# Sample attention of a two-layer decoder step: the value pages from the third on are issued from ACT's DMA queue instead of SP's

## The chip, the cores and the metric

The kernel runs on one core of a Trainium2 chip. The metric is the device time of one execution in microseconds, lower is better. Instructions are written out for each engine: PE (TensorE), DVE (VectorE), ACT (ScalarE), POOL (GpSimd) and SP (SyncE, which here only issues DMAs). Every engine takes its own instructions in order, and engines wait for each other through semaphores.

## The reference

One inference step over a prompt of 512 tokens and eight sample sequences of four new tokens, model width 2048. Layer 0 is a gated linear recurrence, layer 1 a stick-breaking attention with 16 heads, 4 key and value heads and head size 128. The sample sequences attend to 1024 past tokens each, whose keys and values lie in a paged pool; the page table says which eight pages of 128 tokens belong to a sequence.

```python
past_k = cache_k[page_table].reshape(Bs, n_pages * PAGE_SIZE, KV_HEADS, HEAD_DIM)
past_v = cache_v[page_table].reshape(Bs, n_pages * PAGE_SIZE, KV_HEADS, HEAD_DIM)
...
z = jnp.einsum('bqkgd,bskd->bkgqs', qb, k).astype(jnp.float32) / math.sqrt(HEAD_DIM)
z = z + bias.astype(jnp.float32)[None, :, :, None, None]
log_keep = jnp.where(mask, jax.nn.log_sigmoid(-z), 0.0)
suffix = lax.cumsum(log_keep, axis=4, reverse=True) - log_keep
attn = jnp.where(mask, jnp.exp(jax.nn.log_sigmoid(z) + suffix), 0.0)
o = jnp.einsum('bkgqs,bskd->bqkgd', attn.astype(v.dtype), v)
```

The suffix sum runs from the newest token back, so the pages are taken from the newest to the oldest.

## The kernel before

The dense layers come first and last: SP loads weight tiles, ACT and DVE split them into a high and a low part, PE multiplies in three passes (L610 to L612). Between the attention of the prompt and the output projection stands the sample attention, with all eight sequences together. It is the part that the change touches.

The sample attention is a loop of 16 turns, written out, over half pages: turn j works on page n = j // 2 + 1, counted from the newest, and on sequences 0 to 3 (even j) or 4 to 7 (odd j), so on four pages of 128 tokens by 512 numbers. Every engine has its own version of the loop, and stages of different turns stand side by side in it (four turns follow for the tail). Per turn:

- PE transposes four key pages (`key_turn`, L849), each followed by the scores of an earlier one (`scores`, L863), then multiplies the weights of turn j - 4 with its four value pages (`values`, L887) and transposes the weights of turn j - 3 (`weights_turn`, L882). The key pages 4j + 2 to 4j + 5 are transposed in turn j; for 4j + 2 PE needs ACT's copy of page 4j.
- ACT copies even key pages from PSUM to SBUF (`key_copy`, L1219, pages 4j and 4j + 2), does the absolute value, the exponential and the logarithm of turn j - 1 (L1222, L1223, L1226), the exponential of the weights of turn j - 2 (`weight_exp`, L1232), and copies the transposed weights of turn j - 3 from PSUM (`weight_copy`, L1237).
- DVE copies the odd key pages (L1694), scales the logits (L1720) and does the suffix sum (L1725 to L1733).

Pages are kept in two slots (n % 2) for keys (`KPG`) and for values (`VPG`). SP issues all page loads, 256 KB each, four in a group, one group for each half page. For each load it reads the page's number from SBUF into a register (`value_load`, L452) and issues the DMA (L454). The keys and values of pages 1 and 2 are issued first, 32 loads. From page 3 on a key group waits until PE has transposed the half page that it overwrites (`kp_t`), and a value group until PE has multiplied the one that it overwrites (`d_pv`); key groups and value groups alternate, the values two pages behind the keys. `d_pv` counts two for the new tokens and then one for each finished half page of values. After the pages SP goes on with the weights of the output projection (`load_pair_e`, L439).

On ACT two waits ahead of one activation become a semaphore instruction of its sequencer for one and a wait held by the activation for the other; the profile shows it on the line of the second `wait_ge` (L1218, L1236).

Of the kernel before, what the change touches and what calls it, by code (L numbers as in the profile page):

```python
# [33 lines left out]
NB, NT = 8, 4  # L34
# [14 lines left out]
NPAGE = 8  # L49
# [53 lines left out]
def build(nc, a, out):  # L103
    ctx = ExitStack()
    with ctx:
        def sem(name):
            return ctx.enter_context(nc.semaphore(name))
# [4 lines left out]
        def sb(name, shape, dt=F32, offset=None):  # L112
            size = 4
            for n in shape[1:]:
                size *= n
            if offset is None:
                offset = at[0]
                at[0] += (size + 31) // 32 * 32
            return nc.alloc_sbuf_tensor_at(name, list(shape), dt, offset=offset), offset
# [23 lines left out]
        PT, _ = sb("PT", [1, NB * NPAGE], I32)  # L143
# [3 lines left out]
        KPG, _ = sb("KPG", [P, 2, NB, KVW], offset=U_AT)  # L147
        VPG, _ = sb("VPG", [P, 2, NB, KVW], offset=U_AT + 2 * NB * KVW * 4)
# [23 lines left out]
        pt_in = sem("pt_in")  # L172
# [40 lines left out]
        keys_in = [[sem(f"keys_in{n}{h}") for h in range(2)] for n in range(2)]  # L213
        values_in = [[sem(f"values_in{n}{h}") for h in range(2)] for n in range(2)]
# [18 lines left out]
        d_pv = sem("d_pv")  # L233
# [51 lines left out]
        NHALF = 2 * NPAGE  # L285
# [49 lines left out]
        def _(sp):  # L335
# [103 lines left out]
            def load_pair_e(i, strips=(0, 1)):  # L439
                for s in strips:  # L440
                    for u in range(2):
                        load_unit(i * 4 + (E0 + 2 * s + u), u,
                                  w_out_b[:, u * UT:(u + 1) * UT, bass.ds(i * 2 * P + s * P, P)])
# [3 lines left out]
            sp.wait_ge(pt_in, 16)  # L447
            sp.wait_ge(unit_done, E0)

            def load_pages(n, h, pages, cache, arrived):  # L450
                for b in range(h * NB // 2, (h + 1) * NB // 2):
                    page = sp.value_load(PT[0:1, b * NPAGE + NPAGE - n:b * NPAGE + NPAGE - n + 1], min_val=0,  # L452
                                         max_val=cache.shape[0] - 1)
                    sp.dma_start(pages[:, n % 2, b, :], cache[bass.ds(page, 1)].rearrange("o s k d -> s (o k d)"))\  # L454
                        .then_inc(arrived[n % 2][h], 16)

            def load_keys(n, h):
                if n > 2:
                    sp.wait_ge(kp_t, 8 * (n - 3) + 4 * h + 4)
                load_pages(n, h, KPG, a["cache_k"], keys_in)  # L460

            def load_values(n, h):
                if n > 2:
                    sp.wait_ge(d_pv, 2 * (n - 3) + h + 3)
                load_pages(n, h, VPG, a["cache_v"], values_in)

            for n in range(1, 3):
                for h in range(2):
                    load_keys(n, h)
            for n in range(1, 3):  # L470
                for h in range(2):
                    load_values(n, h)
            for n in range(3, NPAGE + 3):
                for h in range(2):
                    if n <= NPAGE:
                        load_keys(n, h)
                    if n > 4:
                        load_values(n - 2, h)
            load_pair_e(0, (1,))
            with sp.Fori(1, KD // 2) as i:  # L480
                load_pair_e(i)
# [484 lines left out]
        def _(act):  # L966
# [248 lines left out]
            def key_copy(c):  # L1215
                act.wait_ge(kp_t, c + 1)
                if c >= 4:
                    act.wait_ge(kp_used, c - 3)  # L1218
                nc.scalar.activation(KPT[:, c % 4, :], KT[:, c % 2], ACT.Copy).then_inc(kp_even, 1)  # L1219

            def one_plus_exp(src, tile):
                steps.done(nc.scalar.activation(tile, src, ACT.Abs))  # L1222
                steps.done(nc.scalar.activation(tile, tile, ACT.Exp, scale=-1.0))  # L1223

            def log_of(tile):
                nc.scalar.activation(tile, tile, ACT.Ln, bias=1.0).then_inc(d_l, 1)  # L1226

            def weight_exp(j):
                act.wait_ge(d_arg, j + 2)
                if j >= 2:  # L1230
                    act.wait_ge(d_wt, j)
                nc.scalar.activation(DW[j % 2], DZ[j % 2], ACT.Exp).then_inc(d_exp, 1)  # L1232

            def weight_copy(j):
                act.wait_ge(d_wt, j + 2)
                act.wait_ge(d_pv, j + 1)  # L1236
                nc.scalar.activation(WPT[:, j % 2, :], WT[:, j % 2], ACT.Copy).then_inc(d_wt_out, 1)  # L1237

            act.wait_ge(d_zout, 1)
            one_plus_exp(new_z, new_l)  # L1240
            log_of(new_l)
            for j in range(NHALF + 4):
                if j < NHALF:
                    key_copy(4 * j)
                if j == 0:
                    act.wait_ge(d_arg, 1)
                    nc.scalar.activation(new_w, new_arg, ACT.Exp).then_inc(d_exp, 1)
                if 1 <= j <= NHALF:
                    act.wait_ge(d_zout, j + 1)
                    if j >= 3:  # L1250
                        act.wait_ge(d_scan, j - 2)
                    one_plus_exp(DZ[(j - 1) % 2], DL[(j - 1) % 2])
                if j < NHALF:
                    key_copy(4 * j + 2)
                if 1 <= j <= NHALF:
                    log_of(DL[(j - 1) % 2])
                if j == 0:
                    act.wait_ge(d_wt, 1)
                    act.wait_ge(d_cleared, 1)
                    for h in range(2):  # L1260
                        nc.scalar.activation(WPT[0:NS, h, :], WT[0:NS, h], ACT.Copy).then_inc(d_wt_out, 1)
                if 2 <= j <= NHALF + 1:
                    weight_exp(j - 2)
                if 3 <= j <= NHALF + 2:
                    weight_copy(j - 3)
            act.wait_ge(d_pv, NHALF + 1)
            nc.scalar.activation(OE[0], OS[:, 0], ACT.Copy).then_inc(d_sums[0], 1)

# [547 lines left out]
```

## Time and profile before

| | us |
|---|---|
| median of 3 runs | 1953.79 |
| lowest, highest | 1953.53, 1960.9 |
| profiled execution | 1958.79 |
| its span | 1957.1 |
| PE busy in the span | 1766.8 (90%) |
| DVE, ACT busy | 1124.3 (57%), 805.7 (41%) |
| page loads, keys and values | 64 + 64 of 256 KB |
| sample attention, first key copy to last value product | 1585.9 to 1709.6 |

Times in the views are microseconds from the span's start. Busy times count an engine's own work; register operations, semaphore waits and DMA issues belong to its sequencer and are shown with a q (SPq, ACTq). The granted clock is given as a share of 2.4 GHz, so 0.50 is 1.2 GHz.

### The profile page before, as it was taken

To read this page: it belongs to the slowest core of one execution; us is meant where nothing else is said; L and a number is where in the kernel's file an instruction comes from. 1 tells how busy PE (TensorE), PEld (TensorE's weight loads), DVE (VectorE), ACT (ScalarE), POOL (GpSimd) and SP (SyncE) were. 2 spreads that over 40 slices of the span, in tenths; PEclk is the share of its full clock that TensorE was granted. 3 is DMA by queue.
4 is the path that set the end of the run, shared out by engine and by line. 5 is a ranking of instruction groups with operands and counts; after the bars stand their busy time and mean duration, and the time that the engine had idled before them with its cause. 6 is when DMAs were issued, how large, how long until landed. Compare 5 with 4: busy or idle time off the path is not lost.

```text
span 1957.1 us, 36289 instructions
## 1 busy us (share of the span) xinstructions
PE 1766.8 (90%) x13985; PEld 1695.8 (87%) x13985; DVE 1124.3 (57%) x1854; ACT 805.7 (41%) x1174; POOL 267.4 (14%) x181
## 2 busy tenths in 40 slices
PE   4899999999997999975889999999999878699995
PEld 3899999999997999974889998999999745499993
DVE  4756565676656222249467666757757757542226
ACT  3344434334445222223255555546545645432212
POOL 3200000000000001014322232232232100001110
PEclk9999999999998999995999999999999979999995
DMA  5332322232221323335312222222222367723324
GB/s 196 94 90 87 93 86 86 86 96 86 75 86 38 92 86 91 91 95 166 92 55 76 66 78 65 65 79 75 65 77 65 98 204 225 229 65 86 86 87 160
DMA packets 278709, 191.67 MB, mean 98 GB/s; under 512 B 7899, under 2 KB 250715, under 8 KB 277979
## 3 DMA queue, kind: packets, MB, share of 16 engines
q1 hardware_dynamic: 277708, 188.03, 32.5%
q0 software_dynamic: 896, 2.23, 0.4%
q8 instruction: 67, 1.10, 0.2%
q14 instruction: 38, 0.31, 0.0%
HBM read 174.26 MB, written 15.97 MB: 97 GB/s over the span
## 4 chain that ended last, share of the span: by engine, by line
PE 71%; DVE 12%; issue 7%; ACT 7%; SPq 2%; DMA 1%; POOL 0%; ACTq 0%; DVEq 0%; POOLq 0%
PE PS L610 20%; PE PS L611 20%; PE PS L612 20%; PE PS L849 1%; PE Z L610 1%; PE Z L611 1%; PE Z L612 1%; DVE Y L1525 1%; ACT L1160 1%; ACT WS L975 1%; DVE T L1567 1%; SPq L452 1%; DMA prow<-in_state_h_dram 1%; DVE T L1565 1%; ACT T L1107 1%
## 5 line engine op out<-in xcount | busy, mean ns | idle before, releaser
L610 PE MATMUL PS<-U,WS 128*128 128x272 f32 x3712 | 1086.6, 293 | 58.9 <-DVE U L1532 34.2
L611 PE MATMUL PS<-U,WS 128*128 128x272 f32 x3712 | 1087.3, 293 | 0.0
L612 PE MATMUL PS<-U,WS 128*128 128x272 f32 x3712 | 1084.8, 292 | 0.0
L610 PEld LDWEIGHTS PS<-U,WS 128*128 128x128 f32 x3712 | 713.4, 192 | 66.3 <-issue 34.3
L612 PEld LDWEIGHTS PS<-U,WS 128*128 128x128 f32 x3712 | 712.8, 192 | 0.0
L611 PEld LDWEIGHTS PS<-U,WS 128*128 128x128 f32 x3712 | 711.3, 192 | 0.8
L1303 DVE TENSOR_TENSOR WS<-raw,WS 128x1024 fp32r<-128x1024 f32 (+1 forms) x240 | 304.5, 1269 | 507.4 <-ACT WS L975 504.9
L975 ACT ACTIVATE WS<-raw 128x1024 fp32r<-128x1024 f32 (+1 forms) x240 | 246.6, 1028 | 605.4 <-PE PS L612 602.0
L527 POOL TENSOR_TENSOR raw<-raw,GN 128x1024 f32<-128x1024 f32 x80 | 160.0, 2000 | 433.5 <-DMA raw<-in_b_w_in_dram 337.7
L539 POOL TENSOR_TENSOR T<-T 128x544 f32<-128x544 f32 x60 | 88.4, 1474 | 379.4 <-ACT T L1071 376.9
L536 POOL COPY T<-T 128x544 f32<-128x544 f32 x4 | 3.0, 744 | 808.8 <-ACT T L1071 781.7
L849 PE MATMUL PS<-IDN,KPG 128*128 128x128 f32 x256 | 45.1, 304 | 21.9 <-ACT KPT L1219 17.6
L1578 DVE TENSOR_TENSOR T<-T,Z 128x256 f32<-128x256 f32 (+1 forms) x64 | 33.3, 520 | 50.9 <-PE Z L749 50.8
L849 PEld LDWEIGHTS PS<-IDN,KPG 128*128 128x128 f32 x256 | 29.4, 151 | 36.1 <-ACT KPT L1219 21.0
L1071 ACT ACTIVATE T<-Y 128x544 f32<-128x544 f32 (+1 forms) x48 | 31.1, 648 | 71.6 <-DVE Y L1503 71.6
L1106 ACT ACTIVATE T<-T 128x256 f32<-128x256 f32 (+1 forms) x64 | 31.7, 495 | 64.8 <-DVE T L1551 64.7
L1134 ACT ACTIVATE U<-T 128x256 fp32r<-128x256 f32 (+1 forms) x64 | 31.9, 499 | 62.9 <-DVE T L1567 62.9
L1124 ACT ACTIVATE U<-T 128x256 fp32r<-128x256 f32 (+1 forms) x64 | 31.7, 495 | 60.9 <-DVE T L1583 60.9
L1572 DVE TENSOR_TENSOR U<-T,U 128x256 fp32r<-128x256 f32 (+1 forms) x64 | 43.3, 677 | 14.9 <-ACT U L1134 14.5
L1398 DVE SCALAR_TENSOR_TENSOR T<-T,CH 128x512 f32<-128x512 f32 x60 | 45.1, 752 | 8.4 <-DVE T L1396 2.9
L770 PE MATMUL Z<-U,KVP 128*128 128x256 f32 (+1 forms) x64 | 24.1, 377 | 27.3 <-DVE U L1588 24.5
L1503 DVE COPY Y<-PS 128x544 f32 (+1 forms) x32 | 23.1, 721 | 41.1 <-PE PS L612 41.1
(221 smaller groups left out, 1972.8 us busy)
## 6 DMA issues: line engine op xcount, KB each, us to landing
raw<-in_a_w_in_dram SPq DMA_DIRECT2D x80, 512.0 KB, 3.8
raw<-in_b_w_in_dram SPq DMA_DIRECT2D x64, 512.0 KB, 4.0
raw<-in_a_w_out_dram SPq DMA_DIRECT2D x32, 512.0 KB, 3.9
raw<-in_b_w_out_dram SPq DMA_DIRECT2D x32, 512.0 KB, 4.0
KPG<-in_cache_k_dram SPq DMA_DIRECT2D x64, 256.0 KB, 3.0
VPG<-in_cache_v_dram SPq DMA_DIRECT2D x64, 256.0 KB, 2.9
T<-scratch_x SPq DMA_DIRECT2D x32, 272.0 KB, 2.9
scratch_x<-T SPq DMA_DIRECT2D x16, 272.0 KB, 2.1
```

Of the source, the lines that this page charges most:

```text
L527: pool.tensor_tensor(raw[:, slot], raw[:, slot], g, ALU.mult).then_inc(w_fold, 1)
L539: ins = pool.tensor_tensor(T[:, 6, 0:TOK], T[:, 6, 0:TOK], sq, ALU.add)
L610: pe.matmul(psum, w_hi, x_hi, start=first, stop=False)
L611: pe.matmul(psum, w_hi, x_lo, start=False, stop=False)
L612: return pe.matmul(psum, w_lo, x_hi, start=False, stop=last)
L849: ins = pe.transpose(KT[:, c % 2, k * P:(k + 1) * P], KPG[:, (j // 2 + 1) % 2, j % 2 * 4 + i, k * DH:(k + 1) * DH], IDN[:])
L975: nc.scalar.activation(WS[:, slot, 0, 0:tiles, :], raw[:, slot, 0:tiles, :], ACT.Copy).then_inc(w_high, 1)
L1134: nc.scalar.activation(U[:, 36, q], T[:, 2, q], ACT.Copy).then_inc(sp_high, 1)
L1303: V.tensor_tensor(WS[:, slot, 1, 0:tiles, :], raw[:, slot, 0:tiles, :], WS[:, slot, 0, 0:tiles, :].bitcast(F32), ALU.subtract).then_inc(w_ ...
L1398: V.scalar_tensor_tensor(xc[:, 0:SEQ], xp[:, k:k + SEQ], param(i, j, k), xc[:, 0:SEQ], ALU.mult, ALU.add)
L1572: V.tensor_tensor(U[:, 37, q], T[:, 2, q], U[:, 36, q].bitcast(F32), ALU.subtract).then_inc(sp_low, 1)
L1578: V.tensor_tensor(T[:, 3, q], T[:, 3, q], later_sum[:, q], ALU.subtract).then_inc(arg_ready, 1)
```

## The change

SP issues all keys and the values of pages 1 and 2, then goes on. The value groups of pages 3 to 8, 12 groups of four loads, are issued by ACT, one in each turn 5 to 16, right behind the weight copy of that turn. A group in turn j waits for `d_pv` to reach j - 2, the value for which the weight copy of that turn also waits. Slots, semaphores and sizes stay as they were.

```diff
+            for n in range(3, NPAGE + 1):
                 for h in range(2):
-                    load_values(n, h)
-            for n in range(3, NPAGE + 3):
-                for h in range(2):
-                    if n <= NPAGE:
-                        load_keys(n, h)
-                    if n > 4:
-                        load_values(n - 2, h)
+                    load_keys(n, h)
             load_pair_e(0, (1,))
...
+            def load_values(j):
+                n, h = j // 2 + 1, j % 2
+                act.wait_ge(d_pv, j - 1)
+                for b in range(h * NB // 2, (h + 1) * NB // 2):
+                    page = act.value_load(PT[0:1, b * NPAGE + NPAGE - n:b * NPAGE + NPAGE - n + 1], min_val=0,
+                                          max_val=a["cache_v"].shape[0] - 1)
+                    act.dma_start(VPG[:, n % 2, b, :], a["cache_v"][bass.ds(page, 1)].rearrange("o s k d -> s (o k d)"))\
+                        .then_inc(values_in[n % 2][h], 16)
+
+            act.wait_ge(pt_in, 16)
...
                 if 3 <= j <= NHALF + 2:
                     weight_copy(j - 3)
+                if 5 <= j <= NHALF:
+                    load_values(j - 1)
```

## Rows read from the trace of the kernel before

**Rows 1.** The page, part 4: the chain that ended last, by engine.

```profile
PE 71%; DVE 12%; issue 7%; ACT 7%; SPq 2%; DMA 1%; POOL 0%; ACTq 0%; DVEq 0%; POOLq 0%
```

**Rows 2.** Stretches: start:end, length, busy time (count) per engine, clock, DMA share, GB/s.

```profile
1618.00:1670.00 52.00, 42.29 (x673) 28.74 (x672) 37.27 (x57) 31.83 (x56) 0.00 (x0) 1.00 0.79 234
1690.00:1710.00 20.00, 10.59 (x219) 7.79 (x219) 9.59 (x15) 9.11 (x17) 0.00 (x0) 0.99 0.81 247
1720.00:1760.00 40.00, 40.00 (x319) 40.00 (x319) 12.83 (x14) 9.33 (x11) 2.34 (x2) 1.00 0.28 79
1651.02:1657.49 6.47, 5.30 (x84) 3.59 (x84) 4.63 (x8) 3.98 (x8) 0.00 (x0) 1.00 0.77 237
```

**Rows 3.** Timeline of ACT: start, length, line, tiles; some first key copies of turns.

```profile
1618.65 0.59 ACT L1219 ACTIVATE KPT<-PS 128x512 f32<-128x512 f32 x1
...
1663.96 0.59 ACT L1219 ACTIVATE KPT<-PS 128x512 f32<-128x512 f32 x1
...
1670.81 0.59 ACT L1219 ACTIVATE KPT<-PS 128x512 f32<-128x512 f32 x1
...
1689.93 0.59 ACT L1219 ACTIVATE KPT<-PS 128x512 f32<-128x512 f32 x1
```

**Rows 4.** Timeline of SP's DMA issues; two groups that follow each other.

```profile
1651.65 3.63 SPq L454 DMA_DIRECT2D KPG<-in_cache_k_dram  x4
1656.05 3.67 SPq L454 DMA_DIRECT2D VPG<-in_cache_v_dram  x4
```

**Rows 5.** Timeline of PE: waits for DMA, in brackets; two of ACT's last weight copies.

```profile
1677.30 1.11 PE L849 MATMUL PS<-IDN,KPG 128*128 128x128 f32 x4 [3.89 <-DMA KPG<-in_cache_k_dram]
...
1695.39 0.58 ACT L1237 ACTIVATE WPT<-Z 128x512 f32<-128x512 f32 x1
...
1705.28 0.60 ACT L1237 ACTIVATE WPT<-Z 128x512 f32<-128x512 f32 x1 [2.22 <-PE Z L882]
1708.53 1.08 PE L887 MATMUL Z<-VPG,WPT 128*32 128x128 f32 x32 [3.29 <-DMA VPG<-in_cache_v_dram]
```

**Rows 6.** Timeline of one steady turn: PE and ACT.

```profile
1651.66 0.66 PE L849 MATMUL PS<-IDN,KPG 128*128 128x128 f32 x4 [1.17 <-ACT KPT L1219]
...
1653.56 0.64 PE L849 MATMUL PS<-IDN,KPG 128*128 128x128 f32 x4
...
1655.94 0.63 ACT L1232 ACTIVATE T<-T 128x512 f32<-128x512 f32 x1 [2.00 <-DVE T L1733]
1656.31 0.66 PE L882 MATMUL Z<-IDN,T 128*128 128x128 f32 x4
1657.00 0.60 ACT L1237 ACTIVATE WPT<-Z 128x512 f32<-128x512 f32 x1 [0.43 <-PE Z L882]
1657.49 0.59 ACT L1219 ACTIVATE KPT<-PS 128x512 f32<-128x512 f32 x1
```

**Rows 7.** Instructions of a page load on SP: count, ns min/median/max, first and last start.

```profile
L452 SPq TENSOR_LOAD <-PT x128: 262/268/463, 1552.1 to 1704.0; - x128
L454 SPq DMA_DIRECT2D VPG<-in_cache_v_dram x64: 337/338/687, 1571.0 to 1704.7; - x64
```

**Rows 8.** ACT's sequencer behind waiting activations; one such activation with its wait.

```profile
L1218 ACTq EVENT_SEMAPHORE  x1: 17/17/17, 1657.0 to 1657.0; - x1
...
L970 ACTq ALU_OP  x1: 35/35/35, 142.3 to 142.3; - x1
...
142.34 1.06 ACT L975 ACTIVATE WS<-raw 128x1024 fp32r<-128x1024 f32 x1 [4.07 <-PE PS L612]
```

**Rows 9.** Clock, a stretch as in rows 2; PE at the lower clock.

```profile
1676.00:1682.00 6.00, 4.70 (x56) 3.41 (x56) 1.91 (x3) 0.36 (x1) 0.00 (x0) 0.50 0.79 233
...
1682.28 0.66 PE L882 MATMUL Z<-IDN,T 128*128 128x128 f32 x4
...
1607.99 1.09 PE L849 MATMUL PS<-IDN,KPG 128*128 128x128 f32 x4 [0.28 <-ACT KPT L1219]
...
1610.99 0.66 PE L882 MATMUL Z<-IDN,T 128*128 128x128 f32 x4
```

More of the change, by code:

```diff
@@ L448, in _ @@
             sp.wait_ge(unit_done, E0)
[L450 to L455, printed above, removed]
             def load_keys(n, h):
@@ L459, in load_keys @@
                     sp.wait_ge(kp_t, 8 * (n - 3) + 4 * h + 4)
[L460 to L465, printed above, removed]
+                for b in range(h * NB // 2, (h + 1) * NB // 2):
+                    page = sp.value_load(PT[0:1, b * NPAGE + NPAGE - n:b * NPAGE + NPAGE - n + 1], min_val=0,
+                                         max_val=a["cache_k"].shape[0] - 1)
+                    sp.dma_start(KPG[:, n % 2, b, :], a["cache_k"][bass.ds(page, 1)].rearrange("o s k d -> s (o k d)"))\
+                        .then_inc(keys_in[n % 2][h], 16)
             for n in range(1, 3):
@@ L470, in _ @@
             for n in range(1, 3):
-                for h in range(2):
-                    load_values(n, h)
-            for n in range(3, NPAGE + 3):
-                for h in range(2):
-                    if n <= NPAGE:
-                        load_keys(n, h)
-                    if n > 4:
-                        load_values(n - 2, h)
+                for b in range(NB):
+                    page = sp.value_load(PT[0:1, b * NPAGE + NPAGE - n:b * NPAGE + NPAGE - n + 1], min_val=0,
+                                         max_val=a["cache_v"].shape[0] - 1)
+                    sp.dma_start(VPG[:, n % 2, b, :], a["cache_v"][bass.ds(page, 1)].rearrange("o s k d -> s (o k d)"))\
+                        .then_inc(values_in[n % 2][b // 4], 16)
+            for n in range(3, NPAGE + 1):
+                for h in range(2):
+                    load_keys(n, h)
             load_pair_e(0, (1,))
@@ L1237, in weight_copy @@
                 nc.scalar.activation(WPT[:, j % 2, :], WT[:, j % 2], ACT.Copy).then_inc(d_wt_out, 1)
+            def load_values(j):
+                n, h = j // 2 + 1, j % 2
+                act.wait_ge(d_pv, j - 1)
+                for b in range(h * NB // 2, (h + 1) * NB // 2):
+                    page = act.value_load(PT[0:1, b * NPAGE + NPAGE - n:b * NPAGE + NPAGE - n + 1], min_val=0,
+                                          max_val=a["cache_v"].shape[0] - 1)
+                    act.dma_start(VPG[:, n % 2, b, :], a["cache_v"][bass.ds(page, 1)].rearrange("o s k d -> s (o k d)"))\
+                        .then_inc(values_in[n % 2][h], 16)
+            act.wait_ge(pt_in, 16)
             act.wait_ge(d_zout, 1)
```

## Prediction, made before the run

> **What bounds the kernel now.** I read the page first. The chain that ended last is 71% PE, and by line it is nearly all the three matmul lines of the dense layers [rows 1]; the change touches none of them. The stretches around the sample attention say where it can act [rows 2]: PE is busy all the time from 1720 us on, but 81% in the steady part (1618 to 1670 us) and 53% in 1690 to 1710, while the DMA share stands near 0.8. So everything is decided between about 1584 and 1710 us.
>
> The kernel walks 16 half pages, and each is one turn of a loop on every engine. Call a turn's first key copy on ACT (L1219, copy 4j) its start. Starts are 6.47 us apart from turn 5 (1618.65) to turn 12 (1663.96), then 6.85 us, and the two turns from 1670.81 to 1689.93 take 19.12 instead of 12.95 [rows 3]. Two questions follow: what makes the 6.47, and what makes the rest.
>
> The rest is SP. Its timeline in the same stretch shows four key loads, then four value loads, a group starting 4.40 us after the last [rows 4]. A turn needs both groups, 8.8 us of issuing, and the loop takes 6.47; SP started ahead and loses 2.4 us each turn. It runs out at 1673 us: PE waits 3.89 us for keys, and at the end 3.29 us for values [rows 5]. Without those waits the ten turns from 1618.65 to 1689.93 (71.28 us) would take 10 x 6.47 = 64.7, so SP costs 6.6 us there.
>
> The 6.47 is a ring of PE and ACT [rows 6]. PE starts at 1651.66, when ACT's key copy of 1651.02 is done; it works without a wait for its four page turns, four score groups, the value product and the weight transpose to 1656.97 (5.30 us busy in every 6.47 [rows 2]); ACT then copies the weights out (L1237, 1657.00) and starts the next key copy at 1657.49; PE, which takes its work in order, begins again. ACT's 2.00 us of idle time ahead of L1232 is no room in this ring: it ends before PE does. What stands between L1237 and the next L1219 on ACT counts in full.
>
> **The change part by part.** *SP's relief.* Twelve groups of values leave SP, which is left with 4.4 us per turn against at least 6.47. Keys are never late: -6.6 us. The end can win 2.5 us at most: the last L1237 was over at 1705.88, and L887 could have run about 0.1 later instead of at 1708.53 [rows 5]. Whether it wins that depends on ACT, below. Afterwards PE is fully busy [rows 2], so weights that SP fetches earlier gain nothing: 0.
>
> *The issue on ACT.* Each turn from 5 to 16 gets four loads right behind L1237: per load the page number's read (0.27), register operations between, and the DMA (0.34) [rows 7]; with all gaps 4.40 us per group of four on SP [rows 4], 1.10 each. The trace shows no load on ACT. A lower bound is the two named pieces alone, 0.61 us each, 2.4 per group; an upper one takes both at the longest that SP shows, 0.46 and 0.69, so 1.10 + 0.19 + 0.35 = 1.64 each, 6.6 per group. Over ten turns these ends are 20 us less and 22 us more. I take SP's 4.40: same instructions, same kind of queue; that it costs nothing or gains is excluded by the order on ACT (below). The first load of a group waits for d_pv, but for a count that L1237 already needed; it adds no wait. Queued behind the loads is the next turn's key copy, for which PE waits.
>
> Can the loads run while L1237 waits for PE? The rows say no [rows 6, 8]. L1237 waits until 1657.00; the semaphore instruction behind it on ACT (L1218), whose count had been reached before, runs at 1657.0, not ahead of it. And in the first layer a plain register operation (L970), which waits for nothing, runs at 142.3, at the start of the activation ahead of it (142.34), which had waited 4.07 us for PE. So ACT's sequencer goes on when an activation begins to execute, but not while it waits. The group starts at L1237's start; 0.49 us of it is hidden behind L1237, and the key copy comes 4.40 - 0.49 = 3.91 us later. The groups of turns 5 to 14 stand ahead of a key copy (starts of turns 6 to 15): 10 x 3.91 = +39.1 us.
>
> A page of the Trainium skill says otherwise: in "Perfetto Trace Analysis", section "DVE / Act Engine Instruction (TENSOR_ADD, Activation, etc)", the instruction is pushed into a wait queue and the sequencer is free for the next while it still waits. By that the loads would hide in ACT's idle time; it is a rival below, and [rows 8] speak against it. On the price, "DMA: Bandwidth & Descriptors", section "Latency and other measured facts", puts tensor_load at a floor of about 600 ns, where the row for SP has 268 ns [rows 7]; by the page each group would be 1.3 us dearer and the sum 13 us larger. The row decides.
>
> *The last turns.* From the start of turn 15 to the end of the last value product it is 1709.61 - 1689.93 = 19.68 us now. With the loads: L1237 at 1695.39, group to 1699.8, Abs, Exp, Ln at 0.66 each to 1701.8, weight exponential, L1237 at 1702.3, group to 1706.7, exponential, L1237 at 1707.25, PE 1707.95 to 1709.6 (product, transpose), L1237 at 1709.65, the last product 1710.35 to 1711.4 [rows 5]. Its pages, issued by 1706.7, land 2.9 us later, in time. That is +1.8 us, and the end's gain isn't had.
>
> *What PE's idle time does.* Now PE idles 1.17 us per turn; then it idles 1.17 + 3.91 = 5.1 us, ten times. After the 3.89 us wait that ended at 1677.30, the granted clock was 0.50 (1.2 GHz) from 1676 to 1682 [rows 9]. The work from there (two page turns with scores, product, transpose) took 1677.30 to 1682.94 [rows 5, 9], 5.64 us; the same work in a steady turn took 1653.56 to 1656.97, 3.41 [rows 6]: +2.2 us. Once early in the loop the fall was shorter: at 1607.99 a page turn took 1.09 us in place of 0.66, and two page turns with scores took until 1610.99 [rows 9], 3.00 us against about 1.9: +1.1. An idle time of 5.1 us each turn is longer than the 3.89, so I expect a fall every turn, at a price between those two: 1.7 us, 10 x 1.7 = +17 us (bounds 0 and 22). DVE's and the other ACT work lies beside PE's and stays hidden.
>
> *Sum.* -6.6 + 39.1 + 1.8 + 17 = +51.3 us. The profiled execution took 1958.79 us (span 1957.1), so it would be 2010.1; the median of the runs shown is 1953.79, 5.0 lower, and gives 2005.1, +2.6%.
>
> **The rivals.**
> - *The clock holds.* The loads cost as above, PE stays at 2.4 GHz: +34.3, 1988.1. For it: PE is idle half of 1690 to 1710 us, with a wait of 3.29 us in it, at a mean clock of 0.99 [rows 2, 5]. Against it: 3.89 us of idle time with a fall [rows 5, 9].
> - *Dearer loads.* The read waits until L1237 has written (+0.5 us per group), or SP and ACT hold each other up when both issue (up to 0.34 per load): 0.3 more per load is 10 x 1.2 = +12, 2017 with the clock term. Nothing in this trace has two such queues at work.
> - *The loads are hidden, faster.* If ACT's sequencer passes a waiting L1237, the group runs from the release of L1232 or earlier, in the 2.00 us of idle time ahead of it. Then only SP's relief is left: -6.6 - 2.5 = -9.1, 1944.7. It decides as soon as less than about 0.9 us of a group stands in the ring (9.1 / 10); for that a group must start 3 us or more ahead of L1237's release. For it: ACT is busy 3.98 of 6.47 us [rows 2], so 2.5 us are free each turn, and issue and execution can overlap. Against it: the register operation that didn't pass a waiting activation [rows 8].
>
> **How the numbers follow.** The forecast 0.60 (its own range 1993 to 2015); the clock holds or mostly holds 0.15; dearer loads 0.17; hidden 0.08. The hidden case and the outer end of the dearer one are left out, which gives 1985 to 2022. A measurement of this kernel can tell about 0.5% (9.8 us). The hidden case's 9.1 lies at this bound, so it is split: faster 0.04, same 0.04, slower 0.92.
>
> **What would show it.** In the changed kernel's profile: SP's group distance grows to the turn's length, and PE has no wait for DMA on L849; starts of turns 6 to 15 are 10.4 us apart plus what the clock adds, about 12; ACT's timeline has a gap of 4.4 us between L1237's start and the next L1219, and PE's wait for L1219 grows from 1.17 to about 5.1 us; the granted clock alternates in 1618 to 1730 us. From 1720 us of before on, the stretches have the same lengths. It is wrong if the TENSOR_LOADs on ACT run while L1237 still waits, if a group takes other than 4.4 us, or if the clock in the loop stays at 1.00.

## The result, and the profile after

| | before | changed |
|---|---|---|
| median, us | 1957.35 (4 runs) | 2012.94 (4 runs) |
| lowest to highest | 1953.53 to 1960.99 | 2008.43 to 2014.26 |
| profiled execution (span) | 1958.79 (1957.1) | 2014.15 (2012.5) |

The changed kernel takes 1.028 times as long, 95% interval 1.0248 to 1.0312: 55.6 us slower. The forecast was 51.3 us slower, 2005.1, in a range of 1985 to 2022. Of the 7.8 us between 2005.1 and 2012.94, 3.6 are the median of the kernel before, which was 1953.79 over three runs when the forecast was made and is 1957.35 with the fourth; the other 4.3 are the change's.

The lines have moved: in the changed kernel the key copy on ACT is L1211, the weight exponential L1224, the weight copy L1229; on PE the page transposes are L841, the scores L855, the value product L879; ACT's page loads are L1235 (number) and L1237 (DMA).

The first place to look is the timeline of ACT over one turn. Columns are start, length, engine and line, operation and tiles, and in brackets the idle time before it and what ended it. It is to be read against [rows 6].

```profile
1675.36 0.60 ACT L1229 ACTIVATE WPT<-Z 128x512 f32<-128x512 f32 x1 [0.85 <-PE Z L874]
1676.04 3.48 ACTq L1237 DMA_DIRECT2D VPG<-in_cache_v_dram  x4
1679.62 0.60 ACT L1211 ACTIVATE KPT<-PS 128x512 f32<-128x512 f32 x1 [3.66 <-issue]
...
1685.69 0.63 ACT L1224 ACTIVATE T<-T 128x512 f32<-128x512 f32 x1 [3.10 <-DVE T L1737]
1687.97 0.60 ACT L1229 ACTIVATE WPT<-Z 128x512 f32<-128x512 f32 x1 [1.64 <-PE Z L874]
1688.64 3.46 ACTq L1237 DMA_DIRECT2D VPG<-in_cache_v_dram  x4
1692.20 0.60 ACT L1211 ACTIVATE KPT<-PS 128x512 f32<-128x512 f32 x1 [3.64 <-issue]
```

The key copy comes 4.26 us after the weight copy where it came 0.49 us after it, and the idle time before it is put down to "issue": ACT waited for nobody, its sequencer was at the loads. The sequencer's own instructions in the first of these turns show when it got there (count, ns min/median/max, first and last start):

```profile
L1235 ACTq TENSOR_LOAD <-PT x1: 284/284/284, 1675.4 to 1675.4; - x1
```

The read begins at 1675.4, the start of L1229 (1675.36), although ACT had been idle for 0.85 us before it. Eleven of the twelve groups begin so, within 0.01 us of the start of L1229; the twelfth begins later, not earlier. That is the order that [rows 8] showed for other instructions. PE's side, timeline of the same turn:

```profile
1674.67 0.66 PE L874 MATMUL Z<-IDN,T 128*128 128x128 f32 x4
1680.27 1.12 PE L841 MATMUL PS<-IDN,KPG 128*128 128x128 f32 x4 [4.94 <-ACT KPT L1211]
1681.32 0.66 PE L855 MATMUL PS<-KPT,QS 128*32 128x128 f32 x8
...
1686.29 1.06 PE L879 MATMUL Z<-VPG,WPT 128*32 128x128 f32 x32
```

PE waits 4.94 us for that copy (1.17 before), and its first transposes then take 1.12 us in place of 0.66: they run at 1.2 GHz (the granted clock is 0.50 from 1679 to 1682). The waits of PE and of SP's queue in the whole sample attention, as sum, times and longest:

```profile
PE PS L841 <- ACT KPT L1211: 56.4, 15, 5.3
PE Z L879 <- ACT WPT L1229: 7.3, 4, 5.0
...
SPq L454 <- PE PS L841: 56.6, 12, 8.5
```

PE has no wait for a DMA left; the two of [rows 5] are gone. SP, which was behind, now waits 56.6 us itself.

The ten turns from the start of turn 5 to that of turn 15 as one stretch, before and after. Columns as in [rows 2]; all 840 matmuls of the ten turns are in both.

```profile
1618.65:1689.93 71.28, 55.33 (x840) 37.36 (x840) 46.34 (x71) 39.79 (x71) 0.00 (x0) 0.95 0.79 233
```

```profile
1619.87:1741.21 121.34, 71.03 (x840) 45.65 (x840) 46.99 (x72) 40.92 (x72) 0.00 (x0) 0.79 0.54 159
```

Here are 50.1 of the 55.4 us between the two spans. Another 4.1 us are in the tail: the last value product ends 23.8 us after the start of turn 15 in place of 19.68, at 1765.02. The remaining 1.2 us were there at the start of turn 5 (1619.87 against 1618.65), ahead of the first load on ACT. From the last value product to the end both take 247.5 us.

### The profile page after: what moved, and what is told of

Same layout as the page of the kernel before. It is cut to its first block, busy times and chain, and to the rows that moved or that the text cites. A ratio compares the mean times of both kernels' runs of the same rounds, so it can differ in the third digit from the quotient of the medians.

```text
span 2012.5 us, 36292 instructions
## 1 busy us (share of the span) xinstructions
PE 1790.1 (89%) x13985; PEld 1709.3 (85%) x13985; DVE 1121.6 (56%) x1854; ACT 807.6 (40%) x1174; POOL 267.8 (13%) x181
## 4 chain that ended last, share of the span: by engine, by line
PE 72%; DVE 11%; issue 7%; ACT 7%; ACTq 2%; DMA 1%; POOL 0%; SPq 0%; DVEq 0%; POOLq 0%
PE PS L602 20%; PE PS L604 20%; PE PS L603 20%; PE PS L841 2%; PE PS L855 1%; PE Z L602 1%; PE Z L603 1%; PE Z L604 1%; DVE Y L1529 1%; ACTq L1237 1%; ACT L1152 1%; ACTq L1235 1%; ACT WS L967 1%; PE Z L879 1%; DMA prow<-in_state_h_dram 1%
## 5 line engine op out<-in xcount | busy, mean ns | idle before, releaser
L841 PE MATMUL PS<-IDN,KPG 128*128 128x128 f32 x256 | 57.3, 365 | 56.5 <-ACT KPT L1211 56.4
L841 PEld LDWEIGHTS PS<-IDN,KPG 128*128 128x128 f32 x256 | 37.5, 183 | 74.6 <-ACT KPT L1211 59.6
L1698 DVE COPY KPT<-PS 128x512 f32<-128x512 f32 x32 | 22.0, 689 | 87.4 <-PE PS L841 87.4
L1582 DVE TENSOR_TENSOR T<-T,Z 128x256 f32<-128x256 f32 (+1 forms) x64 | 33.3, 520 | 55.4 <-PE Z L741 55.3
```

The costliest lines, as they stand in the source:

```text
L841: ins = pe.transpose(KT[:, c % 2, k * P:(k + 1) * P], KPG[:, (j // 2 + 1) % 2, j % 2 * 4 + i, k * DH:(k + 1) * DH], IDN[:])
L1582: V.tensor_tensor(T[:, 3, q], T[:, 3, q], later_sum[:, q], ALU.subtract).then_inc(arg_ready, 1)
```

## The experiments

The kernel before was measured again beside the experiments: its median is 1959.41 beside e1, e3, e4 and e5, and 1956.71 beside e2, e6 and e7. The starts of turn 5 lie anywhere from 1613.5 to 1622.9 us in the profiles of the seven kernels below, although no page load and no matmul ahead of it was changed; so I compare the length of the ten turns between profiles, and whole kernels by their medians. The stretches of the ten turns are gathered here, where 64.73 is ten times 6.47:

| kernel | ten turns, us | PE busy | clock | ratio to before (95%) |
|---|---|---|---|---|
| before | 71.28 | 55.33 | 0.95 | 1 |
| changed | 121.34 | 71.03 | 0.79 | 1.028 (1.0248 to 1.0312) |
| e1, late values not loaded | 64.73 | 52.97 | 1.00 | 0.9955 (0.9932 to 0.9977) |
| e6, register reads only | 123.41 | 72.28 | 0.78 | 1.0273 (1.0257 to 1.0289) |
| e3, PE filled | 109.14 | with filler | 0.94 | 1.0211 (1.0178 to 1.0243) |
| e2, two behind the weight copy | 93.99 | 65.07 | 0.84 | 1.0102 (1.0086 to 1.0118) |
| e4, four behind the logarithm | 75.49 | 58.75 | 0.91 | 1.0034 (1.0017 to 1.0052) |
| e5, three and one | 70.60 | 54.40 | 0.98 | 1.0002 (0.9988 to 1.0016) |
| e7, two behind the logarithm | 64.73 | 52.98 | 1.00 | 0.9959 (0.9945 to 0.9973) |

**What SP's relief is worth alone.**

```diff
-                pe.wait_ge(values_in[slot][h], 64 * (j // 4 + 1))
+                if j < 4:
+                    pe.wait_ge(values_in[slot][h], 64)
...
-                if 5 <= j <= NHALF:
-                    load_values(j - 1)
```

> Edit on the changed kernel: the value pages from the third on are not loaded by anyone and PE does not wait for them (that part of the computation is left out; PE multiplies the old pages). It shows what SP's relief is worth when ACT pays nothing. My theory (SP's issue was behind by 6.6 us in the loop and 2.5 us at the end): 9 us faster than before (8 to 11), turns 6.47 us apart throughout, clock 1.00 in the loop. Rival (the long turns of before came from the transfers and not from issuing): also faster, but with waits for keys left in the loop. Rival (relief is worth nothing): no difference from before.

1949.88 against 1959.41, 9.5 us less by the medians. The ten turns:

```profile
1619.05:1683.78 64.73, 52.97 (x840) 35.95 (x840) 46.32 (x71) 39.82 (x72) 0.00 (x0) 1.00 0.48 142
```

6.55 us less than before in these turns, as worked out. The late values on SP were what made the long turns, and they were worth some 9 us in all (4 to 13 by the interval). But the transfers are gone here too, so whether it is the issuing or the transfers is left to e7. The row also gives a measure of what the clock costs: at 1.00 the 840 matmuls take 52.97 us, in the changed kernel 71.03.

**Is it ACT's sequencer or the second queue?**

```diff
+            act.wait_ge(pt_in, 16)
...
                 if 3 <= j <= NHALF + 2:
                     weight_copy(j - 3)
+                if 5 <= j <= NHALF:
+                    for b in range(8):
+                        act.value_load(PT[0:1, b * NPAGE:b * NPAGE + 1], min_val=0, max_val=a["cache_v"].shape[0] - 1)
```

> Edit on the kernel before: SP issues all pages as before, and ACT only reads eight page numbers into registers behind the weight copy of turns 5 to 16, 8 x 0.54 = 4.3 us, and issues no DMA. My theory (the loss is ACT's sequencer time in the ring, not the second queue and not the transfers): as the changed kernel, 52 to 56 us slower than before, turns 11.6 to 13 us. Rival (DMAs from ACT's queue, or both queues together, are what costs): clearly less than that.

2009.92 against 1956.71: 53.2 us slower. ACT issues no DMA here, SP has all the pages as before, and the ten turns take 123.41 us, as long as in the changed kernel (121.34):

```profile
1663.82 0.60 ACT L1237 ACTIVATE WPT<-Z 128x512 f32<-128x512 f32 x1 [1.90 <-PE Z L882]
1668.14 0.60 ACT L1219 ACTIVATE KPT<-PS 128x512 f32<-128x512 f32 x1 [3.72 <-issue]
```

So neither the queue nor the transfers are needed to explain the loss. Register work of 4.3 us at this place in ACT's program does it. (Lines here are those of the kernel before.)

**Half the dose at the same place.** Two of the four loads go back to SP, whose loop alternates key groups with value pairs again:

```diff
+                    if n > 4:
+                        m = n - 2
+                        sp.wait_ge(d_pv, 2 * (m - 3) + h + 3)
+                        for b in range(4 * h, 4 * h + 2):
...
-                for b in range(h * NB // 2, (h + 1) * NB // 2):
+                for b in range(h * NB // 2 + 2, (h + 1) * NB // 2):
```

> Edit on the changed kernel: of the four value loads of a group from the third page on, two go back to SP (alternating with the key groups as before), two stay on ACT behind the weight copy. It halves the dose at the same place. My theory: the key copy comes 2 x 1.04 - 0.49 + 0.14 = 1.7 us late instead of 3.85, ten turns 17 us; SP has 6.6 us of issue in a turn of 8.2, so its 6.6 us are won; the clock term, which was 18 us for 5.0 us of idle time per turn, is smaller for 2.9 us of idle time, between 5 and 18. In all 16 to 30 us slower than before. Rival (a second DMA queue costs a fixed amount as soon as it is used): as the changed kernel, 55 us slower.

1976.66 against 1956.71: 20.0 us slower, in the expected range; a fixed price of the second queue that would explain the 55 us is excluded. ACT's timeline:

```profile
1653.38 0.60 ACT L1238 ACTIVATE WPT<-Z 128x512 f32<-128x512 f32 x1 [1.14 <-PE Z L883]
1654.06 1.41 ACTq L1246 DMA_DIRECT2D VPG<-in_cache_v_dram  x2
1655.58 0.60 ACT L1220 ACTIVATE KPT<-PS 128x512 f32<-128x512 f32 x1 [1.60 <-issue]
```

The key copy is 2.20 - 0.49 = 1.71 us late. Ten times that, the clock's 65.07 - 52.97 = 12.1 us and 64.73 make 93.9; measured are 93.99. The clock term has not halved with the dose (12.1 after 18.1 us).

**The clock term by itself.** PE gets work for a part of its idle time:

```diff
                 if j >= 3:
                     weights_turn(j - 3)
+                if 5 <= j < NHALF - 1:
+                    for i in range(20):
+                        pe.transpose(WT[:, j % 2, i % 4 * P:(i % 4 + 1) * P], IDN[:], IDN[:])
```

> Edit on the changed kernel: PE does 20 transposes of the identity into an unused PSUM bank behind the weight transpose of turns 5 to 14, some 2.9 us of the 5.0 us in which it idles; nothing waits for them. My theory (17 to 18 us of the loss are PE working at 1.2 GHz after each idle time): the clock stays at 1.00 in the loop, turns are 10.3 us apart instead of 12.1, and the kernel is 37 to 39 us slower than before instead of 55. Rival (the longer turns come from something else than the clock, such as contention): as the changed kernel, 55 us slower.

2003.01 against 1959.41: 43.6 us slower in place of 55.6, so 12 us came back and not 17 to 18. In the profile the clock still fell at the beginning (the four turns from turn 5 on are 10.6 to 13.3 us long), and then held until the end of the ten turns. Four turns from there:

```profile
1670.27:1711.26 40.99, 29.93 (x416) 23.11 (x416) 18.54 (x28) 16.38 (x28) 0.00 (x0) 1.00 0.68 207
```

10.25 us a turn, which is 6.47 and 3.78 for the loads; in the changed kernel it is 12.13. Where the clock stood at 1.00 the expectation of 10.3 us came true, and the difference of 1.9 us per turn is the clock's. The filler did not keep the clock up everywhere. The three turns from 1633.43 to 1670.27 have a clock of 0.74 to 0.86 and take 36.84 us where three of 10.25 would take 30.75, and these 6.1 us are about what the whole kernel won less. The filler itself is not in the way there: PE's timeline in the longest of the three shows it at full speed, and behind it PE still waits for ACT.

```profile
1645.98 1.12 PE L841 MATMUL PS<-IDN,KPG 128*128 128x128 f32 x4 [2.96 <-ACT KPT L1214]
...
1653.84 2.35 PE L922 MATMUL Z<-IDN 128*128 128x128 f32 x20
1659.29 1.12 PE L841 MATMUL PS<-IDN,KPG 128*128 128x128 f32 x4 [3.10 <-ACT KPT L1214]
```

What runs at 1.2 GHz is the page work after the wait. The 20 transposes took 2.35 us and not the expected 2.9, so 2.7 to 3.1 us of idle time were left in each turn; why they let the clock fall in some turns and not in the later ones is not shown.

**The same loads at another place.** All four loads behind the logarithm, ahead of the weight exponential:

```diff
                 if 1 <= j <= NHALF:
                     log_of(DL[(j - 1) % 2])
+                if 5 <= j <= NHALF:
+                    load_values(j - 1)
...
                 if 3 <= j <= NHALF + 2:
                     weight_copy(j - 3)
-                if 5 <= j <= NHALF:
-                    load_values(j - 1)
```

> Edit on the changed kernel: the group of four loads stands behind the logarithm of the turn, ahead of the weight exponential, in place of behind the weight copy. My theory (only what stands between the weight copy and the next key copy counts in full): ACT's sequencer reaches the group 1.85 us after the turn's start, is done at 6.1, the exponential comes 1.2 us late and the next key copy 0.65: ten turns 6.5 us, less SP's 6.6 us, so no difference from before within 3 us, clock 1.00. Rival (ACT's work adds up wherever it stands): 38 to 56 us slower than before.

1964.73 against 1959.41, 5.3 us slower: 50 us of the 55.6 are gone by the place alone, and ACT's total work as the cause is excluded. But I had expected no difference, and by the interval it is 3 to 10 us. The ten turns are 75.49 us. PE was busy 58.75 us, 5.8 more than at full clock; the remaining 5.0 us are 0.5 per turn. That this is near the 0.65 expected from the place is a mean of two kinds of turns: the four with a clock of 0.78 have only PE's old 1.17 us of idle time, and the six at 1.00 are 0.6 to 1.1 us longer than 6.47. PE's timeline shows what I had left out:

```profile
1638.83 0.66 PE L841 MATMUL PS<-IDN,KPG 128*128 128x128 f32 x4 [2.09 <-ACT KPT L1211]
...
1640.84 1.12 PE L841 MATMUL PS<-IDN,KPG 128*128 128x128 f32 x4
```

Here 2.09 us of idle time are followed by transposes at half the clock (0.50 from 1640.80 to 1643.90). It is not so every time: after 2.08 us at 1669.13 the whole turn stays at 1.00. A small delay in this ring can be paid more than once.

**Three and one.**

```diff
                     log_of(DL[(j - 1) % 2])
+                if 5 <= j <= NHALF:
+                    load_values(j - 1, 0, 3)
...
                     weight_exp(j - 2)
+                if 5 <= j <= NHALF:
+                    load_values(j - 1, 3, 4)
...
-                if 5 <= j <= NHALF:
-                    load_values(j - 1)
```

> Edit on the changed kernel: three loads of the group behind the logarithm, the fourth behind the weight exponential, so that each part fits in a stretch in which ACT's sequencer would wait for DVE or PE. My theory: three loads end 5.0 us after the turn's start, the exponential is due at 4.9; the fourth ends at 6.0, the weight copy is due at 5.98. At most 0.1 us per turn, so SP's relief is left: 7 to 9 us faster than before, clock 1.00 in the loop. Rival (each load costs something wherever it stands): slower than before or equal.

1959.73 against 1959.41: no difference from before. All of the loss is gone, but SP's relief isn't left over. The ten turns are 70.60 us, 5.9 over 64.73. PE's busy time says 1.4 of it is the clock. The best turns are 6.65 us long (the fourth load ends after PE has the weights ready), which is 1.8 over ten. And three of the 40 loads of these turns have a DMA instruction of 0.73 to 0.91 us in place of 0.34, one 0.64, together 1.6 us more. That adds up to some 4.9 of the 5.9 us. Of the rest, 0.6 are two loads (turns from 1659.74 and 1680.66) with a pause of 0.3 us among their register instructions; the cause of neither the pauses nor the long DMA instructions is shown. In the timeline one long DMA instruction lengthens the group and delays the exponential:

```profile
1655.20 2.81 ACTq L1237 DMA_DIRECT2D VPG<-in_cache_v_dram  x3
...
1658.12 0.63 ACT L1224 ACTIVATE T<-T 128x512 f32<-128x512 f32 x1 [2.47 <-DVE T L1739]
```

The exponential is put down to DVE, but DVE's release was 0.37 us older; the turn before has 2.10 us of idle time at the same place. My expectation had no slack for such instructions, though the kernel before showed up to 0.69 us for SP's [rows 7].

**Two loads behind the logarithm, two on SP.** The split of e2 with the place of e4: by the expectation 0.9 us of slack on ACT, and 6.6 us of issue per turn on SP. Against e2:

```diff
                     log_of(DL[(j - 1) % 2])
+                if 5 <= j <= NHALF:
+                    load_values(j - 1)
...
                     weight_copy(j - 3)
-                if 5 <= j <= NHALF:
-                    load_values(j - 1)
```

> Edit on the kernel with two loads on each queue: ACT's two stand behind the logarithm, so its sequencer is done 1.85 + 2.1 = 3.95 us after the turn's start, 0.9 us ahead of the weight exponential's release. My theory: nothing of it stands in the ring and one long DMA instruction (0.7 to 0.9 us in place of 0.34) is covered too; SP has 6.6 us per turn and started ahead, so it is never late: turns 6.47 us apart, clock 1.00, 7 to 9 us faster than before, as the kernel without late values. Rival (the long DMA instructions or the interleaving of two queues cost wherever they stand): equal to before.

1948.6 against 1956.71, 8.1 us faster than before (5 to 11 by the interval), some 63 us faster than the changed kernel. The profile shows ACT's loads inside its idle time, and the stretch of the ten turns:

```profile
1654.64 0.62 ACT L1227 ACTIVATE T<-T 128x512 f32<-128x512 f32 x1
1654.82 1.40 ACTq L1246 DMA_DIRECT2D VPG<-in_cache_v_dram  x2
...
1657.26 0.63 ACT L1233 ACTIVATE T<-T 128x512 f32<-128x512 f32 x1 [2.00 <-DVE T L1746]
```

```profile
1613.50:1678.23 64.73, 52.98 (x840) 36.00 (x840) 46.34 (x71) 39.79 (x71) 0.00 (x0) 1.00 0.89 289
```

Each turn is 6.47 us, with the 2.00 us of idle time of [rows 6] unchanged, and the DMA share is 0.89. This also settles what e1 left open: with all the pages transferred, at 289 GB/s, the loop is as fast as with the late values left out. In the long turns of the kernel before, the limit was the issuing and not the transfers.

## Why the prediction was right, step by step

- *SP's relief, -6.6 us in the ten turns.* Right: e1 and e7 both measure 71.28 - 64.73 = 6.55 us. The end's 2.5 us were not had in the changed kernel, as said. They would not have been had in full anyway: from the start of turn 15 to the end of the last value product e1 takes 18.81 us and e7 18.56 where before took 19.68, so 0.9 and 1.1 us. There too PE does some of the last products at 1.2 GHz: two of e1 take 1.94 and 1.93 us, one of e7 1.94.
- *A group on ACT, 4.40 us, key copy 3.91 us late.* Right, slightly high. A load takes 1.04 us on ACT, and from the weight copy's start to the key copy's it is 4.23 to 4.26 us in seven of the ten turns and 4.53 to 4.59 in three. The ten sum to 43.4 us, less 4.9: 38.5 where 39.1 was said. The bounds (20 us less, 22 more) were wider than needed.
- *ACT's sequencer does not pass a waiting activation.* Right: the first read starts with the weight copy, at 1675.4, after ACT's idle time, and so in eleven of twelve groups. The Trainium skill's "Perfetto Trace Analysis", section "DVE / Act Engine Instruction (TENSOR_ADD, Activation, etc)", has the sequencer free as soon as the instruction is in the wait queue. The trace disagrees for the activations seen here, both in front of register operations and in front of loads.
- *PE at 1.2 GHz, +17 us.* Right that PE's work runs at the lower clock: 71.03 - 52.97 = 18.1 us. That the size is so well met is in part luck. The price per turn was a guess between two rows (1.1 and 2.2 us). The mean is 1.8, and e3 shows 1.9, but the single turns lie from nothing (the first, PE busy 5.30 us) to 2.75 (the one from 1716.26, 8.05 us), outside both rows. Summed: 64.73 + 38.5 + 18.1 = 121.3, measured 121.34.
- *The last turns, +1.8 us.* Too low, 4.1 measured. I had counted the loads there and left the clock out. Three of the last four value products take 1.93 us each where they took 1.08 in [rows 5]; the granted clock is 0.50 from 1755 to 1765. That the clock makes the whole difference of 2.3 us is read from these rows, no run shows it by itself:

```profile
1755.52 1.93 PE L879 MATMUL Z<-VPG,WPT 128*32 128x128 f32 x32 [4.97 <-ACT WPT L1229]
...
1763.09 1.93 PE L879 MATMUL Z<-VPG,WPT 128*32 128x128 f32 x32 [0.69 <-ACT WPT L1229]
```

- *The rivals.* The clock did not hold. Dearer loads: excluded, they were cheaper than on SP. Hidden loads, faster than before: not at this place, but the arithmetic behind it (about 9 us for SP's relief once the loads are out of the ring) is what e7 measured (8.1, between 5 and 11).

Of the 4 us between forecast and result, 2.3 are the tail, 1.1 the clock, -0.6 the groups, and 1.2 were there ahead of the loop, where profiles of unchanged code differ by more than that.

## What to carry to other kernels

Moving DMA issues to a compute engine moves sequencer time, a microsecond per load with a register address here, and its price in this loop depended on the place more than on the sum. Between the weight copy and the key copy, where PE waits for the next activation, it counted in full (4.3 us of register work, e6); ahead of an activation that would have waited anyway, two loads cost nothing that the profile shows (e7), and four cost a little, because they did not fit (e4). Look in the timeline for the engine's idle time, find what ends it, and put the issue ahead of the instruction that waits, not behind it, with some slack for a long DMA instruction. And if PE is in the ring, price the idle time twice, once as time and once as matmuls at half the clock, the second with wide bounds: here it was anything from nothing to 2.75 us in a turn.

## What the runs showed of the hardware that I had not expected

- The clock term does not go with the idle time. PE's mean idle time per turn (length less busy time) is 1.2 us in e7, 1.6 in e5, 1.7 in e4, 2.9 in e2 and 5.0 in the changed kernel; PE's extra busy time over the ten turns is 0, 1.4, 5.8, 12.1 and 18.1 us. So e5 and e4 idle alike, and the one pays four times what the other pays. Nor does a single wait decide it. In e5, PE's timeline has a fall right behind a wait of 1.69 us, and full speed behind one of 2.26:

```profile
1624.61 0.66 PE L841 MATMUL PS<-IDN,KPG 128*128 128x128 f32 x4 [1.69 <-ACT KPT L1211]
...
1625.59 1.12 PE L841 MATMUL PS<-IDN,KPG 128*128 128x128 f32 x4
...
1640.07 0.65 PE L841 MATMUL PS<-IDN,KPG 128*128 128x128 f32 x4 [2.26 <-ACT KPT L1211]
```

The turn of the first (1623.96 to 1631.86) has a mean clock of 0.78, that of the second (1639.42 to 1646.07) 1.00. What decides is not shown by these runs, and each of them is one profile.
- A load issued by ACT's sequencer is a little cheaper than one by SP's: 1.04 against 1.10 us, with the DMA instruction itself at 344 against 338 ns. Some DMA instructions take longer, up to 0.9 us on ACT and up to 1.4 us on SP. They are too few to say from these runs what they wait for; some coincide with one of the other queue, some don't. That stays open.
